# Two 64-row end blocks computed as one 128-row product, and the work around the first u reordered

## What is computed

```
u = h * (1.0 + sc1) + sh1            # ada parameters: silu(c) @ w_ada + b_ada
z = u @ w_in                         # q, k, v of 24 heads are columns of z
# pattern 0: half = 64, dil = 1
kb, vb = kblocks(k), kblocks(v)      # keys in blocks of 64, shifted by half a query tile
s = q @ k + bias ; o = softmax(s) @ vb
```

## Time and profile before

| what | value |
|---|---|
| median of three runs | 3949.03 us |
| the profiled execution's own time | 3940.97 us |
| its span | 3939.2 us |
| granted TensorE clock, mean | 0.951 of full speed |
| PE busy | 3636.8 us, 92%, 16076 matmuls |
| PEld, DVE, ACT, POOL busy | 71%, 41%, 34%, 37% |
| chain that ended last | PE 80%, DVE 11%, ACT 4%, POOL 2% |
| HBM | 97 GB/s over the span |

### The profile page before, as it was taken

The page is one execution under the profiler, slowest core; times in us unless marked ns, Lnnn a source line. Parts: engine busy times, 40 slices in busy tenths (PEclk is TensorE's granted clock), DMA queues, the critical chain, the costliest instruction groups (busy, mean ns, idle before and its releaser), DMA issues.

```text
span 3939.2 us, 39173 instructions
## 1 busy us (share of the span) xinstructions
PE 3636.8 (92%) x16076; PEld 2809.5 (71%) x16076; DVE 1618.4 (41%) x2149; ACT 1339.4 (34%) x2169; POOL 1470.9 (37%) x793
## 2 busy tenths in 40 slices
PE   6997989898999999888899899999898999899999
PEld 4786655775888678755577678876466888677887
DVE  2425445436342333355443644325546320454320
ACT  2444234322322244423432232225442332453221
POOL 2332222443545333222334345533223544324443
PEclk9998889999999999889899999999899999999999
DMA  5333111243555333311124355542113433212332
GB/s 186 107 103 102 49 38 38 77 133 120 162 161 154 98 97 113 113 54 43 32 72 123 115 155 171 150 117 73 38 31 98 128 97 96 76 44 82 97 96 75
DMA packets 566978, 385.29 MB, mean 98 GB/s; under 512 B 13598, under 2 KB 504302, under 8 KB 566798
## 3 DMA queue, kind: packets, MB, share of 16 engines
q1 hardware_dynamic: 564574, 379.56, 32.9%
q10 hardware_dynamic: 2224, 3.21, 0.3%
HBM read 379.25 MB, written 2.10 MB: 97 GB/s over the span
## 4 chain that ended last, share of the span: by engine, by line
PE 80%; DVE 11%; ACT 4%; POOL 2%; issue 1%; DMA 1%; SPq 1%; ACTq 0%; DVEq 0%; POOLq 0%
PE ps L174 79%; POOL wlo L144 2%; PE ps L178 1%; DVE mq L152 1%; DVE nrm L149 1%; ACT whi L140 1%; DVE ACC L152 1%; DVE nrd L155 1%; DVE H L152 1%; SPq L171 1%; DVE nrm L144 1%; ACT L136 1%; DVE RR L144 0%; DVE UL L144 0%; DVE ST L158 0%
## 5 line engine op out<-in xcount | busy, mean ns | idle before, releaser
L144 POOL TENSOR_TENSOR wlo<-raw,whi 128x1024 fp32r<-128x1024 f32 (+1 forms) x540 | 1282.6, 2385 | 1945.0 <-ACT whi L140 1944.6
L174 PE MATMUL ps<-UH,whi 128*128 128x512 f32 x2656 | 1068.7, 402 | 65.4 <-ACT UH L140 36.1
L174 PE MATMUL ps<-UH,wlo 128*128 128x512 f32 x2656 | 1051.5, 396 | 22.3 <-POOL wlo L144 22.2
L174 PE MATMUL ps<-UL,whi 128*128 128x512 f32 x2656 | 1051.2, 396 | 5.1 <-DVE UL L144 3.5
L140 ACT ACTIVATE whi<-raw 128x1024 fp32r<-128x1024 f32 (+1 forms) x540 | 546.4, 1023 | 536.9 <-PE ps L174 229.6
L174 PEld LDWEIGHTS ps<-UH,whi 128*128 128x128 f32 x2656 | 507.9, 191 | 188.8 <-ACT UH L140 41.9
L174 PEld LDWEIGHTS ps<-UH,wlo 128*128 128x128 f32 x2656 | 507.7, 191 | 141.2 <-POOL wlo L144 32.5
L174 PEld LDWEIGHTS ps<-UL,whi 128*128 128x128 f32 x2656 | 506.7, 191 | 123.6 <-DVE UL L144 12.8
L152 DVE SCALAR_TENSOR_TENSOR ACC<-raw,SM,ACC 128x512 f32<-128x512 f32 x308 | 370.7, 1204 | 20.2
L174 PE MATMUL ps<-GH,whi 128*128 128x512 f32 x704 | 274.8, 390 | 0.0
L174 PE MATMUL ps<-GL,whi 128*128 128x512 f32 x704 | 274.0, 389 | 0.0
(11 more groups left out here) (322 smaller groups left out, 4251.5 us busy)
## 6 DMA issues: line engine op xcount, KB each, us to landing
raw<-in_w_in SPq DMA_DIRECT2D x168, 512.0 KB, 4.0
raw<-in_w SPq DMA_DIRECT2D x120, 512.0 KB, 5.1
raw<-in_ada_w SPq DMA_DIRECT2D x96, 512.0 KB, 4.6
raw<-in_w_ada SPq DMA_DIRECT2D x80, 512.0 KB, 4.7
raw<-in_ffn_w_gate SPq DMA_DIRECT2D x44, 512.0 KB, 3.8
raw<-in_ffn_w_up SPq DMA_DIRECT2D x44, 512.0 KB, 3.9
raw<-in_ffn_w_down SPq DMA_DIRECT2D x32, 512.0 KB, 3.7
raw<-in_ev_w_in SPq DMA_DIRECT2D x20, 512.0 KB, 3.8
```

The costliest lines, as they stand in the source:

```text
L144: return self.e.tensor_tensor(o, a, b, op).then_inc(*self.done(*keys))
L174: m = self.e.matmul(o, l, r, start=start, stop=stop)
```

## The change

1. Two new tiles `UE` (high and low part, 4 KB a partition each) hold tokens 0 to 63 and 448 to 511 side by side for every kt. ACT writes the high part just ahead of `UH` (`act_hi`), and who writes `UL` writes the low part just ahead of it (`put_lo`), in the norms n0 (layer 0) and n2 (layer 1) only: 8 more ACT copies and 8 more subtractions in each layer, 128 x 128.
2. The two 64-row blocks of V become one of 128 rows, in one PSUM bank: 12 matmuls a kt for V where there were 15. V needs four banks, not five. The last block lands in rows 64 to 127, so the zeros of `VA` block 4 are now in rows 0 to 63, all of `pt` is copied at once (one 128x512 copy where there were one 64x128 and one 128x384) and `pt` needs no zeros.
3. PE waits for `wlo` after the first matmul of a kt in `pe_first`, no longer ahead of it.
4. `act_start`: the order of the copies to `H`, the weight splits and the rounding of u is another; `UH` 0 stands ahead of the splits of chunks 1 and 2, `UH` 1 ahead of chunk 3 and of the copy of the ada rows, and the later splits stand between the roundings.
5. `pool_attention`: the zeros of `VA` come first; the memsets of `pt` and the wait for all `UL` are gone.
6. SP issues the many small vector loads (`v1`) after chunk 7, not after chunk 4.
7. Step P = 0 of layer 0 has no fills. Each later fill call in the program so stands two calls further on.

```diff
+    UE = [at("UEH", 28, [128, NT, 128], F32R), at("UEL", 32, [128, NT, 128], F32R)]
+    def ends(x):
+        return x.rearrange("p (a b) -> p a b", a=8)[:, 0:8:7, :]
...
+    def row_products(p, key, groups, os, k, XH, XL, wh, wl, lo, used):
+        for gr, ((which, blocks), o) in enumerate(zip(groups, os)):
+            xh, xl = (UE[0][:, k, :], UE[1][:, k, :]) if which is ENDS else (XH[:, k, which], XL[:, k, which])
+            p.mm(o[:, :], xh, wh, k == 0, False)
+            if gr == 0:
+                p.wait_ge(*lo)
+            p.mm(o[:, :], xh, wl, False, False)
...
+            p.mm(o[:, :], xl, wh, False, k == NT - 1, *ks)
...
-            if i == 5:
+            if i == 8:
                 vec_loads(s, VECS[3:], "v1")
...
-        for kt in range(3):
+        for kt in range(4):
             turned(kt)
+        rounded(0)
         act_split(a, lin_end["V", 0, 0, "c", 1])
-        for kt in range(3, NT):
+        for kt in range(4, NT):
             turned(kt)
+        rounded(1)
         act_split(a, lin_end["V", 0, 0, "c", 1] + 1)
-        sq = norm_tiles("n0")[0]
-        for kt in range(NT):
-            if kt == 4:
-                act_split(a, lin_end["V", 0, 0, "c", 3] + 1)
-            a.wait_ge(*on("dve", "s", "n0", kt))
-            a.cp(UH[:, kt, :], sq[kt % 2][:, :], ("uh", "n0", kt))
-            if kt in (0, 3):
-                act_first_rows(a, 2 + kt // 3)
+        act_first_rows(a, 2)
+        rounded(2)
+        rounded(3)
+        act_split(a, lin_end["V", 0, 0, "c", 2] - 1)
+        act_first_rows(a, 3)
+        rounded(4)
+        act_split(a, lin_end["V", 0, 0, "c", 3])
+        rounded(5)
+        act_split(a, lin_end["V", 0, 0, "c", 3] + 1)
+        rounded(6)
+        rounded(7)
...
+    def act_hi(a, nid, kt, sq):
+        if nid in ("n0", "n2"):
+            a.wait_ge(*on("pe", *(("adw", 0) if nid == "n0" else ("r1", NT - 1))))
+            a.cp(end_tile(0, kt), ends(sq[kt % 2][:, :]), ("ueh", nid, kt))
+        a.cp(UH[:, kt, :], sq[kt % 2][:, :], ("uh", nid, kt))
+    def put_lo(e, nid, kt, sq):
+        e.wait_ge(*on("act", "uh", nid, kt))
+        if nid in ("n0", "n2"):
+            e.tt(end_tile(1, kt), ends(sq[kt % 2][:, :]), end_tile(0, kt).bitcast(F32), ALU.subtract, ("uel", nid, kt))
+        e.tt(UL[:, kt, :], sq[kt % 2][:, :], UH[:, kt, :].bitcast(F32), ALU.subtract, ("ul", nid, kt))
...
-        return ([(slice(0, 64), 64)] + [(slice(64 + 128 * i, 192 + 128 * i), 128) for i in range(3)]
-                + [(slice(448, 512), 64)])
+        return [(ENDS, [(0, 0, 64), (4, 64, 64)])] + [(slice(128 * i - 64, 128 * i + 64), [(i, 0, 128)]) for i in range(1, 4)]
...
-            if P < 13:
+            if 0 < P + lay and P < 13:
                 pe_fill(p)
```

More of the change, by code:

```diff
@@ L376, in pe_part, with end_tile, row_banks, pe_rows @@
             p.mm(o[:, :], wh, XL[:, k, :], False, k == NT - 1, *([("used", i), key] if k == NT - 1 else []))
-    def pe_rows(p, key, name, lay, c0, blocks, group, emptied_by, XH, XL, xw, between=None):
-        banks = [bank(p, group, key + (i,), emptied_by[i]) for i in range(len(blocks))]
+    WHOLE = [(slice(128 * b, 128 * b + 128), [(b, 0, 128)]) for b in range(4)]
+    ENDS = "ends"
+    UE = [at("UEH", 28, [128, NT, 128], F32R), at("UEL", 32, [128, NT, 128], F32R)]
+    def ends(x):
+        return x.rearrange("p (a b) -> p a b", a=8)[:, 0:8:7, :]
+    def end_tile(w, kt):
+        return UE[w][:, kt, :].rearrange("p (a b) -> p a b", a=2)
+    def row_banks(p, key, groups, banks, emptied_by):
+        os = []
+        for _, blocks in groups:
+            os.append(bank(p, banks, key + (blocks[0][0],), *[emptied_by(i) for i, _, _ in blocks]))
+            for i, _, _ in blocks:
+                bank_of[key + (i,)] = bank_of[key + (blocks[0][0],)]
+        return os
+    def row_products(p, key, groups, os, k, XH, XL, wh, wl, lo, used):
[5 more added lines that the diff above has]
+            p.mm(o[:, :], xh, wl, False, False)
+            ks = (used if gr == len(os) - 1 else []) + ([key + (i,) for i, _, _ in blocks] if k == NT - 1 else [])
+            p.mm(o[:, :], xl, wh, False, k == NT - 1, *ks)
+    def pe_rows(p, key, name, lay, c0, groups, banks, emptied_by, XH, XL, xw, between=None):
+        os = row_banks(p, key, groups, banks, emptied_by)
         for k0 in range(0, NT, 2):
@@ L390, in pe_rows @@
                     p.wait_ge(*xw(k)[1])
[L391 to L399, removed]
+                row_products(p, key, groups, os, k, XH, XL, wh, wl, on("pool", "lo", i),
+                             [("used", i)] if kt else [])
             lin_end[key + ("c", k0 // 2)] = i
@@ L963, in pe_first @@
         bl = v_blocks(0)
-        vb = [bank(p, (0, 1, 2, 3, 4), ("V", lay, 0, i), (v_lane(i), ("VA", lay, 0, i))) for i in range(len(bl))]
+        vb = row_banks(p, ("V", lay, 0), bl, (0, 1, 2, 3), lambda i: (v_lane(i), ("VA", lay, 0, i)))
         qb = [bank(p, (5, 6), ("qk", lay, 0, w), ("act", ("qk", lay, 0, w))) for w in range(2)]
```

95 lines of the change are left out of this document (37 added, 58 removed).

## The result

| | before | after |
|---|---|---|
| median of the runs shown with the result | 3948.46 us (3938.96 to 3949.03, 4 runs) | 3904.30 us (3896.71 to 3909.48, 4 runs) |
| ratio | | 0.9892, 95% interval 0.9869 to 0.9915 |
| span of the profiled execution | 3939.2 us | 3900.5 us |
| granted TensorE clock over the span | 0.951 | 0.955 |

The forecast was 3914 us, with 3901 to 3932 as its range. 38.7 us are gone between the two profiled spans; the terms of the prediction were summed against the profiled execution of the kernel before and gave 35.4.

A forecast was written before the change was run, and what follows sets the result against it. PE's own work (busy 92%) plus its standstills was taken as the bound. Eight terms summed to 35.4 us, taking the profiled 3940.97 us to 3905.6 and the median to 3913.6, forecast 3914; range 3901 to 3932.

The forecast's parts named there:

- Start of u: Layer 0's first product of u starts at about 33.5 us and not 37.72: -4.2 us.
- Waits in `pe_first`: Layer 0: 2.05 us saved before kt 1, 2.3 at kt 4, where about 1 us remains: together -4.3 us.
- its 24 products: Layer 0's V: 24 matmuls fewer at 0.23 us each, -5.5 us.
- restarts: Of three slow restarts of PE after waits (37.72, 48.59, 72.01) one is left: 2 x 1.75 = -3.5 us.
- `VA`: PE's wait for the copies to this tile after `pe_first`: about 2.4 of 5.27 us remain, -2.8 us.
- First steps of attention: Layer 0, no fills in step 0: waits of 1.95 and 1.80 us and a 1.75 us restart go, -5.4 us.
- Layer 1, the merging: Layer 1's V: 24 matmuls fewer, -5.5 us, against extra copies and subtractions, waiting and a later start: sum -4.7 us.
- Narrow products: On PE a 64-wide matmul costs 0.23 us like a 128-wide; rival that merging frees no PE time: chance 0.02, 3925 us.
- Fills two calls further: Layer 0's gating -6.5, feed-forward -3.5; layer 1's +3.8; sum -6.2, taken as -5.0 us.
- the reordering gives nothing: Rival, chance 0.13: u comes earlier but PE stands still at the next thing; only the 48 products go, 3938 us.
- the fills fall badly: Rival, chance 0.15: gating and feed-forward gain nothing, layer 1 loses 3.8 us, two more restarts come: 3927 us.
- slower: Rival, chance 0.03: PE waits for `ACC` at the columns of each fill, 44 pieces at 1.7 us: 3994 us.

The follow-up runs named there:

- experiment 8: Changed kernel plus 16 or 20 products with overwritten results, bridging PE's standstill before the first u after a norm: 3900.3 us, ratio 0.9902.
- experiment 5: Kernel before with the change's queue order, early zeros, fills and small loads, but without the merging: 3911.1 us, ratio 0.9923.
- experiment 3: Changed kernel with the four fill calls of layer 0's first attention step put back: 3917.6 us, ratio 0.9938.
- experiment 2: Changed kernel with ScalarE's queue around the first u in the order of the kernel before: 3920.9 us, ratio 0.9944.
- 7: Kernel before with only the four fill calls of layer 0's first attention step left out: 3930.0 us, ratio 0.9967.
- runs 9 and 10: Changed kernel without layer 1's first-step four fill calls: 3888.0 us, ratio 0.9854; the same with one more call left out in its last step: 3902.1 us, 0.9885.

## Why the prediction was right, and where not

The time came within its range, 10 us below the forecast. Eight of those are no merit or fault of the terms: the sum was moved from the profiled execution (3940.97) up to the median shown then, 3949, and with 17 runs that median is 3942. The unmoved sum, 3905.6, lies on what was measured. That it does is in part luck. Stage by stage the change won 4.3 us in layer 0's mLSTM, 4.4 more than the term in its attention and 9.8 more in layer 1's gating, and lost 3.8, 6.2 and 5.7 us against them in layer 0's feed-forward, layer 1's attention and behind the second feed-forward.

*Start of u* (4.2): 4.2. The steps named are each in the rows: `UL` 0 no longer stretched by POOL, and then the copies to `H` as what is late.

*Waits in `pe_first`, its 24 products, restarts and `VA`* (4.3 + 5.5 + 3.5 + 2.8 = 16.1): the stage went from 60.6 to 45.8 us, 14.8, and to 43.0 where u met the full clock. The wait at kt 4 was given as 1, was 0.84; that for `VA` as 2.4, was 2.66. The terms are not independent, as I had added them: alone the merging gives layer 0 2.4 us by the end of its attention, and the queue order is worth 14.4 us with the merging, since the waits for u grow by what PE no longer has to do (3.26 to 5.66 us before kt 4).

*Restarts* (3.5 here). Off the stage's 14.8 us go 5.5 for the products, 4.5 for the waits at kt 1 and kt 4 and 2.6 for `VA`; 2.2 are left. No run measured the 1.75 us itself. The one start of u at 0.50 clock against one at 1.00 cost 3 us; behind the norm of the feed-forward it cost nothing, as u set the pace. The two ends of the range, 3.6 and 0, were nearer than the middle.

*First steps of attention* (5.4): both waits went. Up to the next wait (138.85 before, 131.54 with the fills alone) that kernel won 6.4 us, and over the whole attention 8.7; the late steps, which I had not costed, gave the rest. The changed kernel won 9.8. Most of that is not waiting time, which two stages show: here are the rows from the tables of stretches (columns as in experiment 8), before and after, for layer 0's attention, and then for layer 1's gating:

```profile
98.32:359.96 261.64, 240.09 (x1379) 203.08 (x1379) 95.28 (x145) 117.70 (x306) 75.84 (x32) 0.94 0.37 109
```
```profile
79.33:331.20 251.87, 232.80 (x1372) 198.04 (x1372) 89.08 (x132) 115.79 (x296) 76.11 (x33) 0.98 0.37 111
```
```profile
2004.19:2258.42 254.23, 231.81 (x977) 182.82 (x977) 122.83 (x117) 69.64 (x92) 109.18 (x50) 0.97 0.40 115
```
```profile
1964.53:2211.71 247.18, 227.41 (x976) 180.02 (x977) 110.02 (x117) 69.62 (x92) 108.87 (x50) 0.98 0.41 118
```

PE stands still for 2.5 us less in the attention (261.64 - 240.09 against 251.87 - 232.80); the other 7.3 of the 9.8 us are busy time, with the clock at 0.98 where it was 0.94. In the gating 2.7 of the 7.0 us are standstill and 4.4 busy time, at 0.98 for 0.97. So where a call falls also decides how long PE works at the lower clock, and the prediction costed that at three restarts only. What in the order of waits makes the clock fall was not tried.

*Layer 1, the merging* (4.7): 4.2, from all but the merge (299.3) to after (295.1). The start is 0.2 us later, the wait 0.79 and not 0.6, at the q tile behind V and for DVE's copy of the values. The rows at the norm confirm the price on GpSimd (timeline of POOL and DVE, after, to be held against the earlier trace rows):

```profile
1321.04 0.84 POOL L144 TENSOR_TENSOR UEL<-nrm,UEH 128x128 fp32r<-128x128 f32 x1 [19.23 <-ACT UH L140]
...
1321.85 1.47 POOL L144 TENSOR_TENSOR UL<-nrm,UH 128x512 fp32r<-128x512 f32 x1
1322.09 1.77 DVE L152 SCALAR_TENSOR_TENSOR H<-H,VT,nrd 128x512 f32<-128x512 f32 x1
...
1325.39 0.84 POOL L144 TENSOR_TENSOR UEL<-nrm,UEH 128x128 fp32r<-128x128 f32 x1 [2.07 <-ACT UH L140]
```

128 columns take 0.84 us there, half of the 1.66 for 512 and between my ends of 0.4 and 1.66. DVE's instruction takes 1.77 us beside POOL's subtraction, where the same one takes 0.74 us elsewhere in this norm, and ends 0.54 us after it: the two still take turns, as the Trainium skill says (SBUF — State Buffer, Who interferes with whom). Two tiles of u come in 4.35 us (forecast 4.6), so PE stayed the bound.

*Narrow products.* That a 64-wide block costs what a 128-wide one does held: 48 fewer were worth 8.2 us of 11, by medians whose intervals overlap, and layer 1's stage is 4.2 us shorter. The Trainium skill (TensorEngine Tiling (Array Packing), Key Properties) says that different tiles of the array can work in parallel. The blocks here, which share one column range, did not; had they, the merging would have brought nothing in experiment 5.

*Fills two calls further* (5.0): in all it was roughly right, but its parts failed. Its size by the runs is the 12.1 to 14.7 us of all fills less the 5.5 forecast or 6.4 measured of the first step, 6 to 9. Layer 0's gating gave 9.0 (6.5). Its feed-forward gave 2.9 with the fills alone (3.5) and 2.6 between experiment 3 and the changed kernel, but nothing between before and after: the changed kernel has a wait of 1.92 us there, 28 us into the stage, that is 0.83 us with the fills alone. That layer 1's gating would lose 2.8 us, since its wait would go from 3.63 to 6.46, was wrong in sign: the wait of 6.26 us came, and the stage got 7.0 us shorter, with less standstill and less low clock in the rows above. I had compared one wait of each stage, the largest. The stages' lengths of the kernel before, 250.4 in layer 0 and 254.2 in layer 1, already said that layer 0's phase was the better one in spite of it. And the attention of layer 1 has a phase too: it is 5.2 us longer in the kernel with the fills alone, with the waits that layer 0's had (4.75 us at its end for 3.17), and I had put that at nothing. Last, from the second feed-forward on 7 us were lost: 416.5 us for its stage and not 414.2, and 971.8 and not 967.2 from the third one's first product (2928.69; before 2971.96) to the end of the span. The kernel with the fills put back has 414.2 and 966.9 again.

*Layer 0's mLSTM stage* gave 4.3 us that no term had. PE stands still for as long as before (41.4 us in both). 1.3 of it lie in its first 33 us and 3.0 behind them, where the clock is 0.89 instead of 0.88 over 315 us. The kernels without the four calls have 346 us there, except the one without the merging (350.6). Why is not shown.

The rivals: "the reordering gives nothing" is out by experiment 2, "the fills fall badly" by 3 and 7, "slower" by the waits of PE for `ACC`, of which only two exceed 0.4 us in the whole trace (1.86 and 5.76 us).

## What to carry to other kernels

Taking work off the engine that is the bound pays only where nothing is late right behind it. The merging alone was worth 0.6 us, and 8.2 with its feeders moved up (each uncertain by some us, as the intervals say). So move the feeders first, or with it, and cost the two together. Where a periodic job is shifted against the stages, compare the lengths of whole stages at each phase and not their largest waits; two layers of one trace may already show them. Then try the phases: one fill call more or less in layer 1 made 14 us between runs 9 and 10, more than the merging was worth.

## What the hardware showed beyond that

PE's clock can fall after PE is back at work, not only in a standstill: with the bridge it went from 1.00 to 0.50 at about 918.8 (0.94 from 917 to 919, 0.50 from 919 to 922), 2.1 us after the first product, which followed a standstill of 2.53 us. And the same instructions can meet either level: 0.50 or 1.00 at 31 to 35 us, 3.3 us of difference. A third place is the stretch from the third mixer's gates to the last but one feed-forward, 174.4 to 174.8 us in four kernels' profiles, 177 in two and 181 in six, with the same waits but for the last one before the product (6.13 us, 5.35 where a piece's columns stand ahead of it, 2.5 with the bridge); the tables of after and of the merging alone:

```profile
2754.10:2928.70 174.60, 155.19 (x557) 97.59 (x557) 79.87 (x117) 74.61 (x92) 30.68 (x41) 0.91 0.07 22
```
```profile
2795.80:2976.80 181.00, 163.31 (x564) 102.29 (x564) 80.28 (x117) 74.90 (x92) 30.90 (x41) 0.88 0.09 27
```

Only the place at 31 to 35 us compares equal instructions; whether the third goes with what each edit moved ahead of it is open, and the changed kernel had 174.6 and 174.7 us in its two profiles. Between them, single profiles can differ by 3 to 10 us away from where an edit acts, and a term of that size needs medians of several runs or the stage in which it acts.
